# Joints worked one token tile at a time, packed narrow weight columns, and DeltaNet's query, key, value product by halves in four banks

## The reference, cut to what matters

```python
h = rms_norm(x, l0_pre);  x = x + rms_norm(gla_mixer(h, ...), l0_post)      # gated linear attention
h = rms_norm(x, l1_pre);  x = x + rms_norm(mla_mixer(h, ...), l1_post)      # 16 heads, latent ranks 512, rope 64
h = rms_norm_2(x, norm1_w);  proj = h @ w_in                                # queries, dn_qkv (3072 columns), gates ...
x = x + (sig(g) * (o_nsa @ w_up_nsa) + sig(g2) * (o_dn @ w_up_dn)) @ w_o    # sparse attention and gated DeltaNet
h2 = rms_norm_2(x, norm2_w);  x = x + (silu(h2 @ w_gate) * (h2 @ w_up)) @ w_down
out = rms_norm_2(x, norm_f)
```

## Time and profile before

| | |
|---|---|
| three runs, median (lowest to highest) | 2390.56 us (2389.57 to 2391.72) |
| the profiled execution | 2388.96 us, of which the profile's span is 2387.2 |
| PE busy | 2332.0 us, 98% |
| DVE, ACT busy | 1467.7 us (61%), 1298.3 us (54%) |
| DMA | 408.94 MB, 171 GB/s on average |
| mean granted PE clock | 0.993 of full |

### The profile page before, as it was taken

How to read it: one execution, slowest core, us unless ns; L and a number is a source line. 1 busy time by engine, 2 the same in 40 slices (tenths; PEclk the granted TensorE clock), 3 DMA queues, 4 the chain that set the end, 5 groups by cost and what they waited for, 6 DMA issues and landing times.

```text
span 2387.2 us, 33365 instructions
## 1 busy us (share of the span) xinstructions
PE 2332.0 (98%) x12514; PEld 1980.5 (83%) x12514; DVE 1467.7 (61%) x2567; ACT 1298.3 (54%) x2397; POOL 18.3 (1%) x38
## 2 busy tenths in 40 slices
PE   8999999899999899999999999999999999999998
PEld 7877788788888899778787888888888888888887
DVE  4554465665565655886777676656666666665554
ACT  5645455565565544775556555546555555554444
POOL 1000000000000000000000000000000000000000
PEclk9999999999999999999999999999999999999999
DMA  6555565556435465656554236656666666665564
GB/s 215 153 167 153 162 204 194 150 151 176 129 118 193 143 185 164 186 169 183 150 168 133 80 98 203 208 180 178 190 188 186 187 189 188 187 205 191 190 190 166
DMA packets 247403, 408.94 MB, mean 171 GB/s; under 512 B 29712, under 2 KB 62528, under 8 KB 246864
## 3 DMA queue, kind: packets, MB, share of 16 engines
q1 hardware_dynamic: 243392, 393.20, 54.4%
q0 software_dynamic: 3136, 10.26, 1.2%
q10 hardware_dynamic: 720, 3.42, 0.4%
HBM read 400.53 MB, written 6.29 MB: 170 GB/s over the span
## 4 chain that ended last, share of the span: by engine, by line
PE 90%; DVE 4%; ACT 4%; issue 1%; DMA 1%; SPq 0%; DVEq 0%; ACTq 0%; POOL 0%; POOLq 0%
PE banks L361 50%; PE banks L335 14%; PE banks L355 9%; PE banks L337 7%; DVE weights_low L306 1%; PE banks L804 1%; ACT weights_high L303 1%; PE banks L644 1%; PE banks L2221 1%; PE banks L2210 1%; PE banks L1681 1%; PE banks L815 0%; DMA weight_ring<-in_w_gla_in 0%; PE banks L1102 0%; PE banks L1112 0%
## 5 line engine op out<-in xcount | busy, mean ns | idle before, releaser
L306 DVE TENSOR_TENSOR weights_low<-weight_ring,weights_high 128x512 fp32r<-128x512 f32 (+3 forms) x1512 | 1006.6, 675 | 831.5 <-ACT weights_high L303 801.4
L303 ACT CAST weights_high<-weight_ring 128x512 fp32r<-128x512 f32 (+3 forms) x1512 | 910.3, 609 | 991.7 <-PE banks L361 624.9
L361 PE MATMUL banks<-weights_high,hidden_T 128*128 128x512 f32 x3008 | 863.9, 399 | 5.8 <-DVE weights_low L306 4.5
L361 PEld LDWEIGHTS banks<-weights_high,hidden_T 128*128 128x128 f32 x3008 | 556.2, 188 | 129.6 <-issue 10.8
L361 PE MATMUL banks<-weights_low,hidden_T 128*128 128x512 f32 x1504 | 466.2, 391 | 0.0
L335 PE MATMUL banks<-hidden_T,weights_high 128*128 128x512 f32 x1408 | 385.1, 394 | 0.6 <-DVE residual L2836 0.6
L361 PEld LDWEIGHTS banks<-weights_low,hidden_T 128*128 128x128 f32 x1504 | 283.0, 188 | 61.4
L335 PEld LDWEIGHTS banks<-hidden_T,weights_high 128*128 128x128 f32 x1408 | 240.4, 189 | 32.9 <-DVE residual L2836 0.8
L337 PEld LDWEIGHTS banks<-hidden_T,weights_low 128*128 128x128 f32 x1408 | 216.5, 189 | 30.3
L337 PE MATMUL banks<-hidden_T,weights_low 128*128 128x256 f32 x1408 | 224.4, 281 | 0.0
L355 PE MATMUL banks<-hidden_T,weights_high 128*128 128x256 f32 (+3 forms) x1120 | 185.8, 287 | 7.3 <-DVE weights_low L306 6.3
(11 more groups left out here) (401 smaller groups left out, 1731.1 us busy)
## 6 DMA issues: line engine op xcount, KB each, us to landing
weight_ring<-in_w_in SPq DMA_DIRECT2D x168, 512.0 KB, 3.6
weight_ring<-in_w_gla_in SPq DMA_DIRECT2D x96, 512.0 KB, 3.8
weight_ring<-in_w_gate SPq DMA_DIRECT2D x88, 512.0 KB, 3.6
weight_ring<-in_w_ffn_up SPq DMA_DIRECT2D x88, 512.0 KB, 3.6
weight_ring<-in_w_down SPq DMA_DIRECT2D x88, 512.0 KB, 3.8
weight_ring<-in_w_mla_in SPq DMA_DIRECT2D x49, 512.0 KB, 3.6
weight_ring<-in_w_gla_out SPq DMA_DIRECT2D x32, 512.0 KB, 3.9
weight_ring<-in_w_mla_out SPq DMA_DIRECT2D x32, 512.0 KB, 4.3
```

Source lines behind the costliest of these rows:

```text
L303: nc.scalar.copy(hi, raw).then_inc(high_ready, 1)
L306: nc.vector.tensor_tensor(lo, raw, hi.bitcast(F32), ALU.subtract).then_inc(low_ready, 1)
L361: last = pe.matmul(ps[:, b + t, 0:width], a[:, t * P:(t + 1) * P], w, start=(k == 0 and n_th == 0), stop=(k == kt - 1 and n_th == 2))
```

## The change

- **Joints per token tile.** The last four k tiles of an output product's last chunk are done first for token tile 0 and then for tile 1 (`first_half`, so far only in the last product). A `PostNorm` makes the factor of each token tile by itself; adds are per quarter and token tile; PE transposes the first tile's blocks while the second's are not there. The four first splits of the next product are put between these steps, and the gain multiplication of the last quarter moves behind two turned groups.
- **Packed columns.** The three narrow weight blocks are laid out by the host as 128 rows, loaded in one transfer and split four k tiles at a time (4 splits, no longer 16); matmuls are the same in number and size. The first is loaded from ACT's queue.
- **The start.** ACT's queue loads the small gain first, then 64 KB of constants (POOL loads the rest, from 6 splits on), then the packed columns; a dummy activation follows. All of `hidden_T` is made ahead of the first wide chunk.
- **prod_dn** is six unrolled chunks; the first keeps its form (the joint uses the other banks), the other five are HALVES_APART. ACT copies one half, DVE adds the other and multiplies by the row. The joint's row moves to another bank.
- **MLA.** Side steps get other slots; the rotation is one instruction per step; PE's wait for the evicted values comes after the first fill of k tiles; k tiles per fill are 2 for 18 calls, none in calls 24 and 30; the gates of chunks 0 and 1 are made right behind the Exp of heads 4 and 8, that of chunk 2 behind the last head.
- **GLA and DeltaNet.** Two groups are transposed 4 and 2 k tiles later; exp and ln steps are two slots apart; in DeltaNet's inversion a subtraction moves ahead of a wait, and a few splits move between fills.

```diff
+        def packed_columns(w, width):
+            def piece(slot, k, n):
+                return slot.rearrange("p a n -> p (a n)")[:, 0:KD * width], w
+            return Gathered(1, piece), KD // PACK, 0, 0, PACK * width, hidden, PACKED
...
+                elif turned == PACKED:
+                    each = width // PACK
+                    for j in range(PACK):
+                        ahi, alo = acts(PACK * k + j)
+                        cs = slice(j * each, (j + 1) * each)
+                        for w, a, n_th in ((hi, ahi, 0), (hi, alo, 1), (lo, ahi, 2)):
...
-                        by_halves = PARTS if first_half is not None and n + 1 == len(self.chunks) else 0
+                        by_halves = PARTS if first_half is not None and i == self.rounds - 1 and n + 1 == len(self.chunks) else 0
...
-                    fill()
+                    if h in late:
+                        late[h]()
+                    else:
+                        fill()
                     nc.scalar.wait_ge(self.turned, h + 1)
...
+            def turn_groups(self, pe, groups, j):
+
                 for t in range(NT):
+                    pe.wait_ge(self.added, NT * j + t + 1)
+                    for g in groups:
+                        last = self.turn.turn_tokens(pe, g, (t,))
+                        if t == NT - 1:
+                            last.then_inc(turned, 1)
...
+                act.wait_ge(first_done, self.n)
+                squares_of(0)
+                after.split(act, 0, 0, 0)
+                self.post.root(0)
+                after.split(act, 0, 0, 1)
+                prod.wait_done(act, prod.rounds - 1, n)
+                squares_of(1)
+                after.split(act, 0, 0, 2)
+                self.post.root(1)
+                after.split(act, 0, 0, 3)
...
+                self.post.inverse(0)
+                after.split(v, 0, 0, 0)
+                self.post.ready(0)
+                self.add(0, 0)
+                after.split(v, 0, 0, 1)
+                self.post.inverse(1)
+                after.split(v, 0, 0, 2)
+                self.post.ready(1)
+                self.add(0, 1)
+                self.add(1, 0)
                 next(self.turns)
+                self.add(1, 1)
+                after.split(v, 0, 0, 3)
                 next(self.turns)
...
-                        if k == (0, 0, 4, 8)[j]:
+                        if k == (0, 0, 1, 2)[j]:
...
-                    pe.wait_ge(low_out, turn0.first + k // 2 + 1)
+                    pe.wait_ge(low_out, turn0.first + 2 * k + 2)
...
-        MO_AT = (17, 19, 21, 23, 25, 27)
+        MO_AT = (19, 21, 23, 25, 27, 29)
+        def mla_tiles(f):
+            return 2 if f < MLA_H + 2 else 0 if f in (24, 30) else 1
...
-        prod_dn = Product([(A["w_in2"], KD, O_DN + n * W, 2 * W, W, hidden, True) for n in range(2)], 3)
+        prod_dn = Product([(A["w_in2"], KD, O_DN + n * W, 0, W) + ((hidden_halves, HALVES_APART) if n else (hidden, True))
+                           for n in range(6)])
...
-                    fill((2, 6)[hf])
+                    fill((3, 5)[hf])
+                for hf in HALVES:
+                    V(v.tensor_tensor(part_of(d_xt, hf), over(ident.unsqueeze(1), [P, NM // 2, P]), part_of(d_ct, hf), ALU.subtract))
...
-            pool.wait_ge(low_ready, KD)
+            pool.wait_ge(low_ready, prod_gla.chunks[0][1] + 2)
...
+            def copy_half(i, n, b):
+                for f in range(2):
+                    Sc(act.copy(dn_raw(n, f), dn_half(n, f, 0)))
+                act.sem_inc(ffn_half, 1)
...
+                v.wait_ge(ffn_half, n)
+                for f in range(2):
+                    V(v.tensor_tensor(dn_raw(n, f), dn_raw(n, f), dn_half(n, f, 1), ALU.add))
+                c = prod_dn.chunk0 + n
+                v.sem_inc(chunk_evicted[c % 2], 1)
+                for f in range(2):
+                    V(v.tensor_tensor(dn_raw(n, f), dn_raw(n, f), row, ALU.mult))
+                return None
...
-            prod_v.wait_evicted(pe)
             mla_attend_tensor(pe)
```

More of the change, by code:

```diff
@@ L27 @@
 PARTS = 4
+PACK = 4
 W = 512
@@ L253, in over, with load_first, load @@
                     body(self.rounds - 1)
-            def load(self, sp):
+            def load_first(self, eng):
+                w = self.chunks[0][0]
+                for n in range(w.pieces):
+                    eng.dma_start(*w.piece(ring[:, self.use0 % SLOTS, :, :], 0, n)).then_inc(landed[self.use0 % SLOTS], 16)
+            def load(self, sp, first=0):
                 def body(i):
-                    u = self.use0
-                    for chunk in self.chunks:
+                    u = self.use0 + first
+                    for chunk in self.chunks[first:]:
                         w, kt, col0, step, width, _, _ = chunk
@@ L498, in body @@
                                 after.prime(eng, side)
-                        if n in which:
+                        if n in which and not (leave_last and final and n + 1 == len(self.chunks)):
                             self.wait_done(eng, i, n)
@@ L641, in turn_group @@
                 for kk in range(2):
-                    for t in range(NT):
+                    for t in tokens:
                         o = kk * S + t * P
                         last = pe.transpose(ps[:, self.bank(g), o:o + P], self.src(t, 2 * g + kk), ident)
-                last.then_inc(turned, 1)
+                return last
             def tensor(self, pe):
@@ L877, in program @@
         n_const = 4 + len(small)
-        const_head = sum(cols[name][1] for name in ("ident", "upto", "after", "ones"))
+        const_head = cols["ident"][1]
         G_K, G_V, G_G, G_LOW = GLA_QK, 2 * GLA_QK, 2 * GLA_QK + GLA_V, 2 * GLA_QK + 2 * GLA_V
@@ L1192, in gla_side_scalar @@
                 act.sem_inc(gk_exp, 1)
-                yield from pace.to(pace.slot + 1)
+                yield from pace.to(pace.slot + 2)
             for kp in range(4):
@@ L1504, in before, with rope_side @@
                     pe.wait_ge(low_out, turn_mo.first + k // 2 + 1)
-            prod_mla_out.tensor(pe, before)
+            prod_mla_out.tensor(pe, before, first_done)
+        def rope_side(ropes, first):
+            pace = Pace()
+            yield from pace.to(first)
+            yield from pace.run(ropes, 4)
         def mla_fill(one, turns):
```

265 lines of the change are left out of this document (159 added, 106 removed).

## The result

The median of the kernel after is 2357.43 us (2355.4 to 2359.2, four runs), against 2391.14 for the kernel before, run beside it (2389.57 to 2391.81). The ratio is 0.9861, 95% interval 0.9846 to 0.9877. The profiled execution took 2355.4 us, its span is 2353.6; against the 2387.2 of before the span is 33.6 us shorter. The forecast was 25.0 shorter, 2365.6: right in direction and inside its range of 2355 to 2379, near its lower end: the forecast time was 8.2 us too high. So the question is where 8.6 us more of span came from, and whether the seven terms are right one by one or only in their sum.

A forecast was written before the change was run, and what follows sets the result against it. PE, busy 2332.0 of 2387.2 us, bounds the kernel, so only its idle time and matmul spacing matter. Seven terms sum to 25.9 us, less 0.9, taken from 2390.6: 2365.6 us, range 2355 to 2379.

The forecast's parts named there:

- DeltaNet's product: In 80 tiles of prod_dn, 8 matmuls replace 12, 0.035 us less each; larger eviction costs zero: 2.8 us.
- The joints: Between products, the next product starts 6.0 us after the old, not 8.0, paced by DVE: 4.0 us for two.
- Rival 2: In the joints, transpose bursts keep the clock at 2.4 GHz: 5.0 us in all, 2360.6; chance 0.13.
- The start: Kernel start: earlier table load and gain let the last packed tile end at 17.0, not 21.80: 4.8 us saved.
- The key rope: MLA's packed key rope: four splits replace 16 small ones that can't keep up: 3.5 us (2.5 to 3.7).
- Other waits for splits: Where side work is moved (exp/ln, rotation, narrow gates), half of 8.3 us of waits goes: 4.2 (0 to 6).
- the inversion: DeltaNet's inversion: two PE waits on a DVE step go as a subtraction and split move: 2.0 us (0 to 2.1).
- The attention: MLA's attention: removed waits and a slow clock stretch, less a new loss: net 4.6 us (1 to 7).
- The terms 1.9, 3.4 and 1.6: MLA's attention savings: wait for evicted values 1.9, Silu ahead of Exp 3.4, half clock after the longer wait 1.6.
- the new loss: MLA's attention, calls 24 and 30 without a k tile: PE waits for Exp, 2.3 us lost.
- The cover of 5.4 us behind the Exp: MLA's attention: a moved Silu has two PE fills, four tiles, 5.4 us, before the next Exp is wanted.
- The 0.9 taken off: Deduction from the summed savings for work moved past waits in five places not followable: 0.9 us (none to 6).
- Rivals 1, 3 and 4: Joints and start stay chain bound (2372.4, 0.17); clock stays low after joints (2399.2, 0.04); attention, side-work waits only move (2374.4, 0.16).

The follow-up runs named there:

- order: Kernel after, with DVE's add of token tile 1's first quarter and ACT's root moved ahead of splits in both joints: 2357.9 us.
- the kernel with the unread matmuls: Kernel after, with matmuls whose results nobody reads (2, 13 and 11) put into PE's three gaps of each joint: 2355.6 us.
- the old Silu: Kernel after, with each Silu of an MLA gate chunk back where its chunk ends, ahead of a head's Exp: 2360.0 us.

## Why the forecast was right, and where it was short

**DeltaNet's product**, 2.8 forecast, 1.5 measured. Mechanism and 1.405 us a tile are right. The step that failed is "about 1 us of cover is left, so the cost is zero". Counted from the chunk's end at 830.20, ACT's copies end at 1.9, not 1.3, since a split stands ahead of them; DVE starts at 2.1 and ends at 5.05, 2.98 us for its four instructions, not 2.6; with the split that is 5.7, where 5.6 was the bound and I had 4.6. And nothing was said of the chunk behind the last one: it is the narrow gates, whose cover would be 1.4 us unpacked, which the measured 5.8 shows.

**The joints**, 4.0 and 5.0. The start of the first k tile was put 6.0 us behind the old product; it is 5.4. PE starts its second transposes at +3.2 where I had +3.3; the error is the last term, 2.7 from transposes to product, which is 2.3. That DVE is the chain was only half right (order). Rival 2, the clock stays up, was false, and the kernel with the unread matmuls shows that its 5.0 would have been 2.4.

**The start**, 4.8 and 3.8 (17.98). ACT's halves begin at 6.72 as said; but groups 4 and up wait for PE's transposes, which now stand between the packed tiles, and ACT idles 1.24 and 0.68 us.

**The key rope**, 3.5 and 3.9. Right: 5.45 us where I had 5.8.

**Other waits for splits**, 4.2 and 10.4, the main error, and it is three. "I take half" was nearly right as a count: of the 8.3 us in the rows of before, 4.7 were in the three stretches (1.3 in GLA, 2.4 around the rotation, 1.0 at the narrow gates) and all of that went, while 3.0 elsewhere stayed. I left out a wait of 1.6 for the gated output (L1234), which the two places 168 and 182 removed, worth 2.1. And I took the rows at face value: the 4.7 cost 8.3. Singly, 0.16 cost 0.3, 0.37 cost 0.63, 1.06 cost 1.33, and 1.6 in four waits cost 3.0. The surcharge is 0.13 to 0.37 us for each wait: the least at the two waits that the old Silu brings back (2.06 in the rows, 2.3 in the stretch), the most in GLA (1.3 in three rows, 2.4 in the stretch). It accounts for most of the inversion too (2.3 in three waits, 3.1 of the 3.4 us), where "2.0 (0 to 2.1)" even excluded what came.

**The attention**, 4.6 and 5.6. The terms 1.9, 3.4 and 1.6 all came, 6.9; the new loss was put at 2.3 in two calls and is 1.3 in one, and 6.9 - 1.3 = 5.6. The cover of 5.4 us behind the Exp held. ACT's rows at head 4 show the switch:

```profile
642.78 1.28 ACT L1523 ACT_TABLE_LOAD   x1
644.08 1.27 ACT L1523 ACTIVATE projections<-banks,statistics 128x512 f32<-128x512 f32 x2
```

The activation starts 1.30 behind the load's start, and PE has no wait at either late Silu. The Trainium skill ("ScalarE: Activation LUTs", "What ACT_TABLE_LOAD costs") has 1.38 more for a drain with each switch. By it, in the forecast's estimate, 1.2 for each of two heads would have come back. The trace disagrees, ahead of the load (ACT ends its work at 642.68) and behind it, and the row was the right choice.

**The 0.9 taken off** for moves that I could not follow was not needed. Rivals 1, 3 and 4 did not come: joints and start together gained 8.8, the clock was back within some 7 us of its fall in each joint, and of the side work only waits of 0.15 to 0.4 us turned up elsewhere.

So the sum came as near as it did in part by luck: the errors of the start and of DeltaNet's product (-1.0 and -1.3) cancel those of the joints, the key rope and the attention (+1.0, +0.4 and +1.0). What is left of the 8.6 is the other waits, 6.2, the inversion, 1.6, and the 0.9 taken off, of which 0.7 was too much. Of these nearly 5 us come from one habit, pricing a wait at its idle time.

## What to carry to other kernels

Price a wait of a pipelined engine by the distance between the starts around it against the same distance without a wait, not by the idle time in its row; here it was nearly 5 us in some sixteen waits. When an eviction grows, look at the chunk behind it: its k tiles are the cover, and narrow ones are four times less. Once a slow clock or one wait is removed, the queue behind it becomes visible, so take the gain of two fixes from a run of both.

## What the runs showed of the hardware

The clock fell to 1.2 GHz while PE was busy without a gap: during the eight decay matmuls that use 16 rows or at most 0.8 us behind them, in before and after alike and in the other eleven traces with these matmuls. In the kernel after they run from 46.87 to 50.56 and the clock is low from 50.9 on, for 3.4 us (6.8 in three of the others). In the one trace with the same columns over 128 rows, 112 of them zero, it stayed at 1.00. I had known it only from idle time.

There is a second such place. Behind or in 32 matmuls of 16 columns (at 1090.60 to 1094.24 in the kernel after) the clock falls in eight of the fourteen traces, for 3.4 us in seven of them and 6.8 in one, though PE is busy and nothing was changed there; in the kernels before and after it doesn't. Such a fall is a difference between executions and no effect of an edit.

How long the clock stays low differs from one execution to the next with nothing changed: in the second joint it was 3.4 or 6.8 us, and from the last matmul of the second layer's product to the broadcast of DeltaNet's row 34.4 to 35.7 us, and 34.3 with the unread matmuls. The Trainium skill says of the ramp at a kernel's start that the number of slow matmuls differs from run to run of the same kernel ("TensorE: Matmul & The Clock Gate", "What's actually happening"); the traces show the like for a slow stretch in the middle of a kernel.

One execution (the tiles spread as before) shows a granted clock of 0.95 in nearly every window, and yet the 28.89 us from the first wide k tile to the decays are the same as in the kernel after, to 0.01. So that figure did not mean slower matmuls.
